# Array halves in turn in the scores and values of two attentions, forget sums added by VectorE, router logits in four column groups, small loads later

## The chip, the cores and the metric

The kernel runs on one core of one Trainium2 chip. Times are device microseconds of one execution, from three runs of the kernel before: the median is 1753.46 us (1751.78 to 1754.30). A profile of one execution gives the rows shown here.

## What is computed

Two transformer blocks on 256 tokens of width 1024, in float32. The first block is a hybrid layer: one projection of the normed input feeds four branches (sliding-window attention "swa" with a relative bias and sinks, a 31-tap convolution, forgetting attention "fox", and block attention "moba" with a relative bias), gated, mixed, and followed by a feed-forward part. The second has a pool branch, a differential attention, a cross attention over 256 memory rows and a mixture of 32 experts of which each token takes four.

```python
# forgetting attention: c is the running sum of log-sigmoid gates
c = jnp.cumsum(log_f, axis=1).transpose(0, 2, 1)
logits = jnp.einsum('bqhd,bshd->bhqs', qi, k) * (HEAD_DIM ** -0.5)
logits = logits + ci[..., None] - c[:, :, None, :]
logits = jnp.where(kpos[None, :] <= qpos[:, None], logits, NEG)
# differential attention: two maps a head, masked by chunks of 64
mask = k_chunk[None, :] <= q_chunk[:, None]
p = jax.nn.softmax(jnp.where(mask, s, -jnp.inf), axis=-1)
a = p[:, :, 0] - lam * p[:, :, 1]
# router
logits = (xt @ w_router + b_router)
top_val, top_idx = lax.top_k(logits, TOP_K)
```

Each of swa, moba and fox has 8 heads of 64 channels, the differential attention 4 heads of two maps with 64 channels each.

## The kernel before

All five engines run programs written out by hand: `tensor_program` (PE), `scalar_program` (ACT), `vector_program` (DVE), `gpsimd_program` (POOL) and `sync_program` (the DMA queue of SP). Each engine works strictly in the order of its program. Between engines there are counting semaphores: `dve["normed", kind, n]` names a step, `q.wait_ge(*...)` waits for it. `Banks` hands out the eight PSUM banks in a fixed turn; `banks.take` waits until the last reader of a bank is through.

Activations lie as channels on partitions, tokens on columns (`h`, `hs`), 8 tiles of 128 x 256. A big weight arrives in "units" of 1 MB (8 x 128 x 256 floats) in four ring slots, issued by SP in the order of the dict `units`, each as soon as PE has finished the unit that held the slot. ACT rounds each unit to a reduced format (`high_r`), DVE computes the rest (`slot_ring_r`, function `rest`), and PE multiplies three times (`thrice`: hi x hi, hi x lo, lo x hi), 48 matmuls of 256 columns a unit. `ahead(name)` on ACT and DVE splits units up to two ahead of the one that PE works on. Scores, values and transposes are plain fp32 matmuls, each of which the trace shows as two records.

The start: ACT issues all 18 loads of small parameter rows (`rows_sb`, L1535), SP loads the identity, x, the first unit, then the constants (L1267, L1268), then further units. POOL issues loads of small inputs. PE transposes x and the rows, norms, and then projects `ub` 0 to 3, `qa` 0 and 1, the forget gate, `ka`/`va`, and q, k, v of moba ("d") and fox ("c").

First attention (`for n in range(8)`): for each head number n PE runs `scores` of swa, moba and fox, a gate unit `gz` 2n, three transposes of each normalised map (`turn_probs`), the unit `gz` 2n+1, and `values` of the three. DVE adds bias or mask (`maxima`, L1896), takes maxima, normalises (`normalise`); ACT takes exponents (`exponents`). Between them DVE does the 31 taps of the convolution and its norm (`conv_step`). A head of 64 channels lies on partitions 0 to 63 or 64 to 127; all three kinds use the same half for the same n. Fox adds its gate sums by a second matmul on two rows (`fox_l` with the sums c, `fox_rt` with -c, rows filled by 16 small DMAs of POOL). POOL also loads a bias matrix `toep` for each swa and moba head from `diag_dram`.

Second block: DVE and ACT norm (`sqrt_table` loads ACT's square-root table), PE projects, rotates, and computes `dscores`: for each head and map m two score matmuls, and after each one a matmul of the identity with the mask `chunk1` that adds it. DVE applies `final_g`, the first block's last norm, to x just ahead of the maxima of the differential attention, and handles the maps one after the other. Then follow `uv`, transposes, pooling, `out2` with its residual (`add_residual`), cross attention, and the router (`wrt`, 8 matmuls into 32 partitions). The experts' weights (12 MB each) come through up to 15 slots; `gate_up` and `down` use 64 columns of the array at a time, in alternating halves, and `scatter` 64 rows at a time.

## Time and profile before

| | us |
|---|---|
| median of three runs | 1753.46 |
| profiled execution | 1753.44 |
| its span, first to last instruction | 1751.6 |
| PE busy in the span | 1607.4 |
| DVE busy | 751.4 |
| ACT busy | 483.4 |
| POOL busy | 166.6 |

The page gives busy time by engine, forty slices of the span with the granted clock of PE and the use of DMA, and the chain of work that ended last. The windows view gives the same for chosen stretches, the timeline single instructions with the idle time before them in square brackets and what ended it. PE is a matmul, PEld a weight load, SPq, ACTq and POOLq the issuing of DMAs. A matmul row shows the array's used rows and columns (64*128: 64 rows, 128 columns), and the size of the moving operand.

### The profile page before, as it was taken

Reading aid. Unit: us, or ns where it says so; the run is one execution under the profiler, and the core shown is the slowest. Engines: PE = TensorE matmul, PEld = TensorE weight load, DVE = VectorE, ACT = ScalarE, POOL = GpSimd, SP = SyncE. Lnnn points to the kernel's source line nnn. Section 1 sums busy time; section 2 is a strip of 40 time slices with the busy share of each in tenths; the row PEclk is TensorE's granted clock in tenths of the full one; section 3 lists DMA queues with packets and bytes.
Section 4 is the critical chain, followed back from the end, with each engine's and each line's share of the span. In section 5 each row is a group of like instructions: output and inputs, shape, how many; then the busy total and the mean of one; then the engine's idle time right before and its main releaser. Section 6 shows DMA issues by size and latency. Waiting matters only on the chain.

```text
span 1751.6 us, 22754 instructions
## 1 busy us (share of the span) xinstructions
PE 1607.4 (92%) x9732; PEld 1015.8 (58%) x9732; DVE 751.4 (43%) x1330; ACT 483.4 (28%) x822; POOL 166.6 (10%) x199
## 2 busy tenths in 40 slices
PE   6999999999999999989999898988888888888885
PEld 6899889989999989984333232323232322323221
DVE  6798765788894678643122121212121212111112
ACT  4445655446554536532011010101010101010001
POOL 1200001503540040110000000000000000000000
PEclk9999999999999999998999999999999999999998
DMA  8754334546655534656999999999999999999994
GB/s 200 204 178 156 117 112 146 167 145 184 183 188 189 179 121 152 221 219 262 405 426 426 426 427 426 425 426 425 426 427 426 426 427 426 426 426 427 427 426 196
DMA packets 194553, 526.44 MB, mean 301 GB/s; under 512 B 18745, under 2 KB 136542, under 8 KB 145294
## 3 DMA queue, kind: packets, MB, share of 16 engines
q1 hardware_dynamic: 190720, 519.34, 76.3%
q0 software_dynamic: 3184, 5.37, 1.6%
q8 instruction: 78, 1.28, 0.3%
q10 hardware_dynamic: 542, 0.21, 0.0%
q14 instruction: 29, 0.24, 0.0%
HBM read 523.24 MB, written 1.61 MB: 300 GB/s over the span
## 4 chain that ended last, share of the span: by engine, by line
PE 43%; DMA 42%; DVE 9%; ACT 3%; issue 1%; SPq 1%; ACTq 1%; DVEq 0%
PE bank L600 42%; DMA slot_ring<-in_w_down 16%; DMA slot_memx<-in_w_down 10%; DMA slot_late<-in_w_down 8%; DMA slot_high<-in_w_down 8%; DVE slot_ring_r L1896 2%; ACT high_r L1479 1%; DVE conv L1904 1%; SPq L1262 1%; ACTq L1535 1%; ACT dscore L1479 0%; DVE rstd L1938 0%; DVE rot_tmp L2330 0%; DMA slot_ring<-in_w_in 0%; DVE x_sb L1904 0%
## 5 line engine op out<-in xcount | busy, mean ns | idle before, releaser
L1896 DVE TENSOR_TENSOR slot_ring_r<-slot_ring,high_r 128x1024 fp32r<-128x1024 f32 x198 | 247.1, 1290 | 96.7 <-ACT high_r L1479 94.2
L600 PE MATMUL bank<-h_hi_r,high_r 128*128 128x256 f32 x1000 | 286.4, 286 | 1.5 <-DVE slot_ring_r L1896 1.3
L600 PE MATMUL bank<-h_lo_r,high_r 128*128 128x256 f32 x1000 | 283.5, 284 | 0.0
L1900 DVE TENSOR_SCALAR ga<-bank 128x512 f32<-128x512 f32 x32 | 22.1, 692 | 579.6 <-PE bank L600 579.6
L600 PE MATMUL bank<-h_hi_r,slot_ring_r 128*128 128x256 f32 x952 | 269.9, 283 | 0.0
L1479 ACT ACTIVATE high_r<-slot_ring 128x1024 fp32r<-128x1024 f32 x198 | 198.0, 1052 | 61.6 <-PE bank L600 42.0
L600 PEld LDWEIGHTS bank<-h_hi_r,high_r 128*128 128x128 f32 x1000 | 191.5, 192 | 4.3 <-DVE slot_ring_r L1896 2.4
L600 PEld LDWEIGHTS bank<-h_lo_r,high_r 128*128 128x128 f32 x1000 | 191.8, 192 | 0.1
L1479 ACT ACTIVATE th_e<-ga 128x512 f32<-128x512 f32 x32 | 20.2, 630 | 612.4 <-DVE ga L1900 612.4
L600 PEld LDWEIGHTS bank<-h_hi_r,slot_ring_r 128*128 128x128 f32 x952 | 182.5, 192 | 0.0
L600 PE MATMUL bank<-slot_ring,xg 128*64 128x512 f32 x528 | 124.6, 604 | 11.7 <-DMA slot_ring<-in_w_gu 11.7
L600 PE MATMUL bank<-slot_high,xg 128*64 128x512 f32 x400 | 94.1, 600 | 7.8 <-DMA slot_high<-in_w_gu 7.8
L1468 POOL CAST bias_of_r<-owners_r 128x128 fp32r<-128x128 f32 x32 | 9.3, 293 | 835.1 <-PE bank L600 835.0
L600 PE MATMUL bank<-slot_ring,hbT 128*64 128x512 f32 x304 | 73.3, 602 | 15.1 <-DMA slot_ring<-in_w_down 15.1
L600 PEld LDWEIGHTS bank<-slot_ring,xg 128*64 128x64 f32 x528 | 34.4, 137 | 88.6 <-issue 51.3
L1900 DVE TENSOR_SCALAR seT_r<-bank,const_sb 128x256 fp32r<-128x256 f32 x32 | 15.5, 484 | 155.1 <-PE bank L600 155.1
L600 PE MATMUL bank<-slot_last,xg 128*64 128x512 f32 x304 | 70.6, 599 | 5.5 <-DMA slot_last<-in_w_gu 5.5
L1479 ACT ACTIVATE hbT<-bank 128x512 f32<-128x512 f32 x32 | 19.1, 597 | 176.0 <-PE bank L1123 176.0
L600 PE MATMUL bank<-slot_late,xg 128*64 128x512 f32 x256 | 61.4, 601 | 5.7 <-DMA slot_late<-in_w_gu 5.7
L600 PEld LDWEIGHTS bank<-slot_high,xg 128*64 128x64 f32 x400 | 25.9, 136 | 66.7 <-issue 38.3
L600 PEld LDWEIGHTS bank<-slot_ring,hbT 128*64 128x64 f32 x304 | 19.9, 136 | 67.5 <-issue 38.4
L600 PE MATMUL bank<-slot_high,hbT 128*64 128x512 f32 x200 | 48.2, 602 | 9.7 <-DMA slot_high<-in_w_down 9.7
(433 smaller groups left out, 2912.1 us busy)
## 6 DMA issues: line engine op xcount, KB each, us to landing
slot_ring<-in_w_gu SPq DMA_DIRECT2D x66, 1024.0 KB, 26.3
slot_high<-in_w_gu SPq DMA_DIRECT2D x50, 1024.0 KB, 26.7
slot_ring<-in_w_down SPq DMA_DIRECT2D x49, 1024.0 KB, 26.5
slot_last<-in_w_gu SPq DMA_DIRECT2D x38, 1024.0 KB, 26.7
slot_ring<-in_w_in SPq DMA_DIRECT2D x36, 1024.0 KB, 5.0
slot_late<-in_w_gu SPq DMA_DIRECT2D x32, 1024.0 KB, 26.4
slot_high<-in_w_down SPq DMA_DIRECT2D x25, 1024.0 KB, 26.9
slot_ring<-in_w_up SPq DMA_DIRECT2D x44, 512.0 KB, 4.5
```

Source lines behind the costliest of these rows:

```text
L600: return e.matmul(o, lhs, rhs, start=start, stop=stop, skip_group_check=True)
L1262: e.dma_start(view(slot_f[slot]), src).then_inc(*slot_in[slot].step("unit", name))
L1468: e.tensor_copy(bias_of[n % 2].rearrange("p (c s) -> p c s", c=2), owners[:, :, n:n + 1].broadcast_to([P, 2, CAP])).then_inc(*pool.step("b ...
L1479: return e.activation(o, i, f, **k)
L1535: e.dma_start(rows_sb[r:r + n, t * P:(t + 1) * P], flat.rearrange("(r p) -> r p", p=P)).then_inc(*rows_ins[t].step("rows"))
L1896: return e.tensor_tensor(o, i, j, op)
L1900: return e.tensor_scalar(o, i, s1, None, op1)
L1904: return e.scalar_tensor_tensor(out=o, in0=i, scalar=s, in1=j, op0=op1, op1=op2)
```

## The change

- **Scores and values, first attention.** One function handles the three kinds of head n. moba uses head n^1, so its half of the partitions is the other one than swa's and fox's. The six score matmuls go in the order swa, moba, fox (256 wide), moba, swa, fox (128 wide), the six value matmuls likewise. The two-row matmuls of fox are gone.
- **Forget sums.** PE transposes the sums to columns (`forget_cols`). POOL stores the negated rows to DRAM (`fox_dram`), loads them for each head broadcast over 128 partitions into one of two buffers `fox_row`, waits for the landing, and adds the causal mask. DVE adds the column and the row in one `scalar_tensor_tensor` in place of the mask's `tensor_tensor`.
- **Differential attention.** Both maps' 256 wide score matmuls, then both 128 wide. The mask matmuls and `chunk1` are gone; DVE writes -1e30 into the unseen quarter of each part in PSUM with one memset a map. The maxima of head n+1 stand ahead of the difference of head n. `final_g` is applied in the `out2` residuals, two of eight tiles ahead of each.
- **Router.** The 8 matmuls go to four groups of 32 partitions, two in each; a matmul with the constant `stack` turns and adds the four.
- **Small loads and steps later.** SP loads the constants ahead of `qa` 0 instead of `ub` 1; the diagonal matmuls come after `qa` 1, their two copies on DVE after the second tap step; POOL's loads of lambda, router and position inputs come after the diagonal stores; ACT spreads the row loads; the rows' second transposes stand between the halves of `ub` 0; ACT's root of `gain_sq` and the square-root table come ahead of the meeting at "block2" instead of behind it.

```diff
@@ scores and values @@
+            def scores(n):
+                for kind in KINDS:
+                    banks.take(q, ("scores", kind, n))
...
+                for kind, i in ((SWA, 0), (MOBA, 0), (FOX, 0), (MOBA, 1), (SWA, 1), (FOX, 1)):
+                    pair, r = n // 2, half_of(kind, n)
...
+                    m = matmul(b[:, c], qt[:, qs], kt[:, ks], True, True)
+                    if i:
+                        m.then_inc(*pe.step("scores", kind, n))
-                for c, qs, ks in ((PARTS[0], slice(128, 256), slice(0, 256)), (PARTS[1], slice(0, 128), slice(0, 128))):
-                    m = matmul(b[:, c], qt[:, qs], kt[:, ks], True, kind != "fox")
-                    if kind == "fox":
-                        m = matmul(b[:, c], fox_pair(fox_l, n)[:, qs], fox_pair(fox_rt, n)[:, ks], False, True)
...
+                for kind, kb in ((SWA, 0), (MOBA, 0), (FOX, 0), (MOBA, 1), (SWA, 1), (FOX, 1)):
+                    r = half_of(kind, n)
+                    o = bank(("heads", kind, pair))[r, 0:S]
...
+                    q.wait_ge(*act["probs", kind, n])
@@ tensor_program, ahead of the q, k, v units @@
+            banks.take(q, "forget columns")
+            q.wait_ge(*dve["forget rows"])
+            for t in range(TT):
+                m = e.transpose(bank("forget columns")[:, t * FOX_H:(t + 1) * FOX_H], zz[:, t * P:(t + 1) * P], ident[0:FOX_H, 0:FOX_H])
@@ differential attention, tensor_program @@
             for head in range(DIFF_H):
+                for c, qs, ks in ((PARTS[0], slice(128, 256), slice(0, 256)), (PARTS[1], slice(0, 128), slice(0, 128))):
+                    for m in range(2):
+                        name, r = ("dscores", head, m), slice(m * HD, (m + 1) * HD)
+                        last = matmul(bank(name)[:, c], uq[r, head, qs], uk[r, head, ks], True, True)
-                        matmul(bank(name)[:, c], uq[r, head, qs], uk[r, head, ks], True, False)
-                        last = matmul(bank(name)[:, c], ident, C("chunk1")[:, cs], False, True)
@@ router @@
-                m = matmul(b[0:NE, 0:S], wrt[:, k, :], h[:, k, :], k == 0, k == KT - 1)
+                m = matmul(b[k % 4 * NE:(k % 4 + 1) * NE, 0:S], wrt[:, k, :], h[:, k, :], k < 4, k >= 4)
-                            m = e.transpose(b[:, S + s * NE:S + (s + 1) * NE], mean_sb[0:NE, s * P:(s + 1) * P], ident[0:NE, 0:NE])
+                            m = matmul(b[:, S + s * NE:S + (s + 1) * NE], mean_sb[:, s * P:(s + 1) * P], C("stack"), True, True)
@@ sync_program @@
-                if name == ("ub", 1):
+                if name == ("qa", 0):
                     e.dma_start(diag_const, a["consts"][:, n_const:]).then_inc(*rest_in.step("rest"))
                     e.dma_start(const_sb[:, 2 * P:], a["consts"][:, 2 * P:n_const]).then_inc(*rest_in.step("rest"))
@@ gpsimd_program @@
+            def fox_rows(n):
+                row = fox_row[n % 2]
+                if n >= 2:
+                    q.wait_ge(*dve["biased", FOX, n - 2])
+                q.wait_ge(*fox_out["fox"])
+                for c, w in ((0, S), (S, P)):
+                    e.dma_start(row[:, c:c + w], fox_dram[n:n + 1, 0:w].broadcast_to([P, w])).then_inc(*fox_ins[n % 2].step("fox", n))
+                q.wait_ge(*fox_ins[n % 2]["fox", n])
...
+                e.tensor_tensor(masked, masked, C("causal")[:, P:2 * P].rearrange("p (c k) -> p c k", c=1).broadcast_to([P, 2, P]),
+                                ALU.add).then_inc(*pool.step("fox", n))
...
                 e.dma_start(toep[n % 8], src).then_inc(*toep_in[n % 8].step("toep", n))
+                if n == 7:
+                    fox_rows(0)
+                    fox_rows(1)
+                elif n >= 9 and n % 2:
+                    fox_rows(n // 2 - 2)
@@ scalar_program @@
+            load_rows(0)
             q.wait_ge(*first_in["first"])
             sqrt_table()
+            load_rows(3)
+            load_rows(2)
...
             for i in (1, 3):
                 evac(("x", i), x[:, 2 * i:2 * i + 2, :], two_of(("x", i)), ("x", i))
+            load_rows(1)
             round_h("ln1_g", range(0, KT // 2))
...
+            sqrt_table()
+            q.wait_ge(*dve["gain squares"])
+            af(gain_sq, gain_sq, ACT.Sqrt).then_inc(*act.step("gain root"))
+            q.wait_ge(*act["gain root"])
             act.mark("block2")
             after_all(q, "block2")
-            sqrt_table()
@@ vector_program @@
-            e.memset(fox_l, 1.0).then_inc(*dve.step())
-            e.memset(fox_rt, 1.0).then_inc(*dve.step())
...
+                    if kind == "fox":
+                        stt(sc[:, c], b[:, c], forget_cols[:, t * FOX_H + n:t * FOX_H + n + 1], fox_row[n % 2][:, c], ALU.add,
+                            ALU.add).then_inc(*dve.step("biased", kind, n))
...
                     ahead((w, i))
+                    if norm == "xattn_g":
+                        q.wait_ge(*act["square", "final_g", 3])
+                        apply("final_g", x, x, steps=(2 * i, 2 * i + 1))
+                        own()
                     q.wait_ge(*pe[w, i])
...
-            q.wait_ge(*act["square", "final_g", 3])
-            apply("final_g", x, x)
...
+            def dmaxima(head):
+                for m in range(2):
+                    b, st = bank(("dscores", head, m)), stats[2 * head + m]
+                    q.wait_ge(*pe["dscores", head, m])
+                    unseen = b[0:CHUNK, P:3 * P].rearrange("p (c k) -> p c k", c=2)[:, :, CHUNK:P]
+                    e.memset(unseen, NEG).then_inc(*dve.step())
+                    own()
...
+            dmaxima(0)
+            for head in range(DIFF_H):
+                if head + 1 < DIFF_H:
+                    dmaxima(head + 1)
+                difference(head)
```

## Rows read from the trace of the kernel before

**Rows 1.** The page: the span.

```profile
span 1751.6 us, 22754 instructions
```

**Rows 2.** Windows: PE, PEld, DVE, ACT, POOL busy (count), granted clock, DMA share, GB/s.

```profile
800.00:805.00 5.00, 4.41 (x28) 2.94 (x30) 3.35 (x14) 1.39 (x3) 0.00 (x0) 1.00 0.01 3
...
837.00:1700.00 863.00, 772.91 (x3544) 263.65 (x3542) 146.12 (x252) 73.58 (x117) 8.71 (x29) 1.00 1.01 426
```

**Rows 3.** The chain that ended last, the start: at us, us long, what.

```profile
8.68 2.32 ACTq L1535
...
20.32 15.26 PE bank L600 x100
...
47.41 6.65 DMA slot_ring<-in_w_in
...
84.14 66.68 PE bank L600 x544
```

**Rows 4.** Timeline of PE, heads 3, 6, 7: start, length, engine, line, out<-in, shapes.

```profile
209.68 0.27 PE L774 MATMUL bank<-const_sb,score_swa 128*128 128x128 f32 x1
...
253.96 0.86 PE L600 MATMUL bank<-prob_swa,va 128*64 128x256 f32 x4
...
256.05 0.70 PE L600 MATMUL bank<-ka,qa 64*128 64x256 f32 x2
...
259.66 0.28 PE L600 MATMUL bank<-h_lo_r,high_r 128*128 128x256 f32 x1
...
284.65 0.27 PE L774 MATMUL bank<-const_sb,score_swa 128*128 128x128 f32 x1
```

**Rows 5.** Timeline of PE in the expert stage: scatter, then gate and up.

```profile
881.88 0.73 PE L600 MATMUL bank<-y_hi_r,seT_r 64*128 64x512 f32 x4
...
882.91 0.39 PE L600 MATMUL bank<-rows_e_r,owners_r 64*128 64x512 f32 x1
...
883.91 1.94 PE L600 MATMUL bank<-slot_memx,xg 128*64 128x512 f32 x8
```

**Rows 6.** Timeline of DVE: last step of heads 0 to 3, first and last of head 4.

```profile
148.71 0.55 DVE L1900 TENSOR_SCALAR score_fox<-score_fox,stat 128x256 f32<-128x256 f32 x2
...
168.08 0.55 DVE L1900 TENSOR_SCALAR score_fox<-score_fox,stat 128x256 f32<-128x256 f32 x2
...
189.12 0.55 DVE L1900 TENSOR_SCALAR score_fox<-score_fox,stat 128x256 f32<-128x256 f32 x2
...
208.05 0.55 DVE L1900 TENSOR_SCALAR score_fox<-score_fox,stat 128x256 f32<-128x256 f32 x2
...
219.51 0.62 DVE L1896 TENSOR_TENSOR score_swa<-bank,toep 128x256 f32<-128x256 f32 x2 [0.49 <-PE bank L600]
...
225.66 0.55 DVE L1900 TENSOR_SCALAR score_fox<-score_fox,stat 128x256 f32<-128x256 f32 x2
```

**Rows 7.** A window in the first attention, columns as in Rows 2.

```profile
240.00:245.00 5.00, 5.00 (x30) 5.00 (x31) 4.16 (x17) 3.79 (x13) 0.00 (x0) 0.66 0.00 0
```

**Rows 8.** DMA issues: out<-in, queue, count, KB each, median us to landing.

```profile
toep<-diag_dram POOLq DMA_DIRECT2D x16, 128.0 KB, 3.1
```

**Rows 9.** Timeline of the differential attention and the out2 stage, PE and DVE.

```profile
637.36 0.70 PE L600 MATMUL bank<-uk,uq 64*128 64x256 f32 x2
...
638.21 3.26 DVE L1904 SCALAR_TENSOR_TENSOR x_sb<-x_sb,cols_sb,rstd 128x256 f32<-128x256 f32 x8
...
653.90 0.37 PE L600 MATMUL bank<-high_r,h_hi_r 128*128 128x256 f32 x1
...
664.23 0.35 DVE L1904 SCALAR_TENSOR_TENSOR dscore<-dscore,stat,dscore 128x128 f32<-128x128 f32 x1
...
697.01 1.52 DVE L1896 TENSOR_TENSOR slot_ring_r<-slot_ring,high_r 128x1024 fp32r<-128x1024 f32 x1 [1.65 <-ACT high_r L1479]
```

**Rows 10.** Timeline of ACT where the second block starts.

```profile
579.32 1.28 ACT L1479 ACT_TABLE_LOAD   x1 [5.65 <-DVE x_sb L1904]
```

**Rows 11.** Timeline of PE, the router.

```profile
787.10 6.52 PE L600 MATMUL bank<-h_sb,wrt 128*32 128x256 f32 x16 [3.14 <-DVE h_sb L1904]
```

## What I predicted, before the change had run

> **What bounds the kernel now.** I read the page first, then the windows, the waits of PE, the chain, and last the timelines of the stages that the change touches. The page gives a span of 1751.6 us [rows 1]; the profiled execution took 1753.44, so 1.84 us lie around the span, and the median of the three runs, 1753.46, is the same number. From 837 us on DMA is busy throughout and moves 426 GB/s while experts are computed [rows 2]: there the end is set by the stream of expert weights, and nothing that PE does in that stretch matters. But the stream can only run ahead as far as there are free slots. At 800 to 805 us DMA stands at 0.01: all slots are full and wait for the router and the first expert [rows 2]. So whatever brings the start of the expert stage forward brings the saturated stream forward by the same, and the end with it. Up to there PE sets the pace: the chain has one piece of PE from 84.14 for 66.68 us and goes on so through the first block [rows 3], and no wait of PE is listed between 140 and 322 us. Before 84 us it is weight loads and VectorE, between 636 and 705 us PE and the softmax chain together. Each part of the change is costed against that.
>
> **Start (moved loads).** ScalarE issues eighteen small DMAs before its first work; the one at 8.68 alone holds its queue for 2.32 us, and PE's first projection starts at 20.32 [rows 3]. After the change eight issues stand ahead, the other ten are spread; six of them (about 0.4 to 0.8 us each in that view) still stand ahead of the rounding of h. SP issues the two constant loads after four weight units instead of after one, and the router's, rotary and lambda loads wait on the POOL queue behind the two diagonal stores. PE's start comes 1 to 3 us earlier. But what comes next in the chain is the DMA of the third unit behind, 6.65 us from 47.41 [rows 3], fed by the 256-byte pieces of the two qa units; the constants now share DMA with these. I take 2.5 us, bounds 0 and 5. The diagonal matmul (1.4 us of PE) and its two copies (1.0 us of DVE) move to the stretch where DVE is late; the two memsets that go (0.96 us) pay for the copies. PE's new wait for "forget rows" before two transposes falls into a gap of 2.6 us that PE has at 82 us anyway; if that cover is gone it costs up to 1.5 us, which is in the bounds. ScalarE's gain root leaves this stage at no cost.
>
> **First attention.** For one head of each kind, values take PE from 253.96 to 256.05, 2.1 us, and scores from 256.05 to 259.5, 3.4 us [rows 4]. By their columns (0.65 us for a 256 and a 128 wide fp32 pair) the scores would be 1.3 us for swa and moba and 1.3 for fox with its two-row matmuls; the 0.8 us more is the switching of fox between 64 rows and 2 rows. The fox matmuls on two rows go altogether, and the six that remain alternate between halves of the array. That halves overlap, rows show: eight 512-column records of y on 64 rows start within 1.03 us, where 0.213 each would be 1.7, and eight records of fp32 on 64 columns take 1.94, where 3.4 would be in sequence [rows 5]. With pairs A, B, A, B, A, A both groups come to 1.28 us; I take 1.45 each for the ends. So PE's own work falls by 2.6 us a head, 21 us in all.
>
> PE will not get all of it. DVE and ScalarE carry a chain from scores to the last normalised fox map of 6.7 us (219.51 to 226.2) [rows 6], and swa's map is now complete 1.07 us after the first score matmul instead of 0.64. In heads 0 to 3 the DVE also does the conv taps and norm: from normalised fox to the next it takes 19.4, 21.0 and 18.9 us (148.71, 168.08, 189.12, 208.05) [rows 6], with hardly a wait for PE, and PE's transposes of head 3 come at 209.68 [rows 4], 1.1 us after the map is ready. So through head 3 only some 1.2 us are gained. From head 4 on the period is 0.4 (rest of the transposes) + 5.7 (48 matmuls) + 1.45 (values) + 1.25 (swa's scores) + 6.7 + 0.1 = 15.6 us; before it was (284.65 - 209.68) / 4 = 18.7 [rows 4], among them three stretches like 240 to 245, where the granted clock is 0.66, partly at 1.2 GHz, right behind half-array matmuls [rows 7]. Four periods give 12.5 us. The last values give 0.7. Against it stand POOL's masks of the fox rows, which share time with DVE: 0.2 us a head, 1.6 us. Together 13 us, bounds 7 and 19. The stt of DVE that adds the column and the row replaces a tensor_tensor of the same shape at the same cost. Behind POOL's new waits for landed rows stand the toep loads of later heads; a toep load lands in 3.1 us [rows 8], POOL adds below 1 us, and each row has over a period of lead, so I cost them at nothing.
>
> On what a switch costs, the dscores show it best: one map there takes 2.07 us on average ((653.90 - 637.36) / 8) [rows 9] for 1.28 us of columns, because each 64-row matmul is followed by one on 128 rows. The Trainium skill, "TensorEngine Tiling (Array Packing)", Key Properties, says that changing the tiling mode drains the array while different tiles of one mode run independently; by it the alternation costs nothing, and its rule agrees with the scatter rows. But the Trainium skill, "TensorE: Matmul & The Clock Gate", Part 3, also says that weight loads overlap running matmuls only where the row group differs; by that the values, which differ in columns alone, would gain nothing, 5 us less. The expert matmuls on 64 columns [rows 5] speak against it.
>
> **Block 2 starts.** At 579.32 ScalarE loads the square-root table for 1.28 us and runs a dummy of 0.1, in the chain, after all engines have met [rows 10]. The change does it before the meeting, where ScalarE has been idle for 5.65 us. Gain 1.4 us.
>
> **Diff attention.** Four things at once. The mask matmuls go: PE needs 0.85 us a head instead of 4.1, 3.4 instead of 16.5 us [rows 9]. DVE no longer applies final_g here (1.75 + 3.26 us at 638.21) [rows 9]. The maxima of the next head run ahead of the difference, so ScalarE's exponents are covered. And two memsets and their waits a head are new on DVE, unseen in this trace: between 0.1 (memset of a small tile) and 0.4 us (a pass over 256 columns), I take 0.2. DVE starts at 638.4, needs 1.8 us for maxima and 2.2 for a difference per head, and ends at 654.4; before it ended at 664.6 [rows 9]. PE gets to uv at 641 and to the transposes at 652.5 instead of 665.5, and waits there for DVE. POOL's pooling starts 3.3 us earlier too and ends at 655.6, just in time. Gain 10.2 us. What is late next is DVE in the out2 stage, where it now has final_g: 1.75 + 8 x 0.42 + three waits, 5.4 us. DVE has idle pieces there such as 1.65 us at 697 [rows 9]; counted unit by unit some 2.6 us are absorbed, and the last residual, on which PE and the next norm wait, comes 2.8 us later. Net 7.4 us, bounds 3 and 11.
>
> **Router.** Eight logical matmuls of 32 columns take 6.52 us [rows 11] at the low clock, while h arrives every 0.41 us. In four column groups the last may start 2.9 us after the first and ends 0.85 later: 2.8 us less, of which I leave 0.5 for a clock that is still low at the transposes behind. Gain 2.3, bounds 0.5 and 3.
>
> **Sum.** 2.5 + 13 + 1.4 + 7.4 + 2.3 = 26.6 us. Span 1725.0, time 1727 us.
>
> **Rivals.** (a) The halves do not overlap for fp32 on 64 rows: every switch of halves costs 0.2 us as in dscores. Scores then take 3.1 us, swa's map is ready 1.5 us later, four periods are 17.1: 6 us less, and 3.5 us less in diff attention: 1736. For it: no fp32 row pair stands in this trace. Against: the scatter. Chance 0.10. (b) The DVE and ScalarE chain gives less than counted, because POOL's masks and the row loads slow DVE, or final_g falls wholly on the out2 stage: 7 us in attention or 5 us in out2: 1734. Chance 0.17. (c) The clock stays at 2.4 GHz in stretches where it fell, and the start gains its 5 us: 1719. Chance 0.12. (d) The kernel gets slower: POOL holds a row pair from "biased" of head n-2 over two loads and an add to head n. Two buffers are in flight, so the period of a head is at least half that path. To lose the 13.6 us of the other parts, eight periods would have to be 1.7 us above today's 18.7, 20.4 us, a path of 41 us. It decides from 31 us on (a period of 15.6). Loads that land in 3.1 us speak against it. At 45 us of path: 1758. Chance 0.02. (e) The stream hides what PE gains, because something ahead of 837 us is bound by DMA after all: within 0.2% of now. Against it: DMA idle at 800. Chance 0.02. The forecast has the remaining 0.57.
>
> **Range and chances.** The unknown costs reach from about 1714 to 1741 if most fall to one side; (a) to (c) lie within that, (d) and (e) outside. A difference of 0.2% is about what a measurement of this kernel can tell. Faster 0.96, same 0.02, slower 0.02.
>
> **What the profile after would show.** Six score matmuls in some 1.4 us; the transposes of head 7 about 16 us before 284.65 with short waits of PE for DVE in front of most fox transposes; no low clock in attention; dscores in under 4 us; the last difference some 10 us nearer to the last upool matmul; DVE without idle time between the out2 residuals; router matmuls in under 4.5 us; the DMA gap at the same depth but earlier. I am wrong if scores still take over 2.5 us, if PE's waits in attention exceed 1 us a head after head 3, if DVE waits for POOL at the fox scores, or if the expert stage starts earlier and the end doesn't follow.

## The result, and the profile of the changed kernel

The changed kernel takes 1744.1 us (median of 7 runs, 1738.2 to 1748.6), the kernel before 1753.9 beside it (7 runs, 1750.8 to 1757.8). The ratio is 0.9946, 95% interval 0.9935 to 0.9958. So it is faster, by 9.7 us or 0.5%, where 26.6 us were forecast, and its time lies outside the range of 1714 to 1741.

The page of the changed kernel, beginning with the span; the last two lines are the DMA engines' busy share and what they moved, in 40 slices of 43.6 us:

```profile
span 1742.7 us, 22667 instructions
...
PEclk9999999999999998999999999999999999999998
DMA  8865455456655544757999999999999999999995
GB/s 221 186 206 146 124 149 169 146 168 183 184 193 179 191 143 136 265 197 291 422 421 421 421 421 421 421 421 421 421 421 422 421 421 423 420 421 422 421 421 216
```

The span is 8.9 us shorter than in [rows 1]. The last line holds the surprise. While the experts are computed the stream moves 420 to 423 GB/s in every full slice, where [rows 2] had 426. The window that answers to the second line of [rows 2] says the same (PE, PEld, DVE, ACT, POOL busy, granted clock, DMA share, GB/s):

```profile
837.00:1700.00 863.00, 761.57 (x3484) 259.02 (x3482) 142.81 (x247) 71.65 (x114) 8.71 (x29) 1.00 1.01 421
```

The DMA share is 1.01 in both: the DMA engines are as busy as before, and each byte takes longer.

The chain that ended last, second block, router and first experts (at us, us long, what):

```profile
591.32 33.09 PE bank L604 x264
...
686.99 31.86 PE bank L604 x244
...
745.66 19.55 PE bank L604 x162
...
770.90 3.61 PE bank L604 x16
...
781.80 18.41 PE bank L604 x82
...
817.22 23.86 PE bank L604 x115
```

The same piece of the first expert (23.86 us, 115 records) began at 834.89 in the kernel before. So the expert stage starts 17.7 us earlier, and the end comes 8.9 us earlier. From that piece to the end of the span it was 1751.6 - 834.9 = 916.7 us; now it is 925.5. Two things have to be explained: 17.7 where 26.6 were forecast, and 8.8 us lost behind that point.

PE in the first attention, head 1: the transposes of its three maps, and the values behind them (start, length, engine, line, operands; in brackets the wait and who ended it):

```profile
163.44 0.30 PE L779 MATMUL bank<-const_sb,score_swa 128*128 128x128 f32 x1 [0.27 <-DVE score_swa L1930]
...
165.31 0.33 PE L779 MATMUL bank<-const_sb,score_moba 128*128 128x128 f32 x1 [1.34 <-DVE score_moba L1930]
...
166.46 0.33 PE L779 MATMUL bank<-const_sb,score_fox 128*128 128x128 f32 x1 [0.60 <-DVE score_fox L1930]
...
168.28 0.58 PE L604 MATMUL bank<-h_hi_r,high_r 128*128 128x256 f32 x1 [1.09 <-ACT gate L1503]
...
176.36 1.89 PE L604 MATMUL bank<-glu,const_sb 128*128 128x256 f32 x8
178.18 0.43 PE L604 MATMUL bank<-prob_swa,va 128*64 128x256 f32 x1
178.19 0.43 PE L604 MATMUL bank<-prob_moba,vd 128*64 128x256 f32 x1
```

Two value matmuls in different halves of the array start 0.01 us apart and run side by side, which is what the change is about. But the transposes wait for VectorE, and from the first fox transpose to the values it takes 11.7 us, where head 2 takes 6.1 (three transposes and 48 matmuls at the full clock). Three things lie in it: a wait of 1.09 us for ScalarE, eight more matmuls, which sum the squares of the convolution for its norm and stand here in head 1 (1.8 us, `glu`), and the clock. Windows of the 5 us before the clock fell and of the 6.8 us in which it was low, of the 5 us steps around them, of one in head 2, and of the end of the out2 stage:

```profile
161.70:166.70 5.00, 2.78 (x15) 1.82 (x14) 4.16 (x17) 3.67 (x14) 1.73 (x3) 1.00 0.92 271
166.70:173.50 6.80, 5.71 (x27) 5.32 (x26) 3.81 (x4) 5.93 (x10) 1.70 (x1) 0.50 0.25 25
...
165.00:170.00 5.00, 3.01 (x14) 2.37 (x15) 4.34 (x9) 4.71 (x10) 0.92 (x2) 0.67 0.68 133
170.00:175.00 5.00, 5.00 (x31) 5.00 (x31) 1.79 (x3) 4.40 (x7) 1.15 (x1) 0.65 0.02 3
190.00:195.00 5.00, 5.00 (x44) 4.96 (x43) 3.84 (x6) 2.53 (x8) 0.53 (x1) 1.00 0.69 226
...
680.00:685.00 5.00, 1.18 (x3) 1.03 (x4) 4.96 (x5) 0.00 (x0) 3.50 (x4) 0.71 0.66 215
685.00:690.00 5.00, 3.88 (x13) 2.80 (x12) 1.63 (x4) 1.19 (x3) 2.68 (x6) 0.50 0.34 101
690.00:695.00 5.00, 5.00 (x35) 5.00 (x35) 4.96 (x11) 2.15 (x6) 0.00 (x0) 0.77 0.00 0
```

Read the PE busy time and the granted clock together. In the 5 us in front of 166.7 PE was busy for 2.78 us, in pieces with waits of up to 1.34 us between them; then the granted clock is 0.50, the lower of its two levels (1.2 of 2.4 GHz), for 6.8 us, into a stretch in which PE has work all the time (170 to 175). The same happens at 680 to 695, with VectorE busy for 4.96 us of the first five. Idle time is not the only thing that a fall follows: in the kernel before the clock falls at 240.0 [rows 7] behind 5 us in which PE was busy throughout:

```profile
235.00:240.00 5.00, 5.00 (x28) 3.50 (x26) 2.33 (x9) 1.26 (x6) 0.00 (x0) 1.00 0.67 210
```

What VectorE of the changed kernel does around 680 us (timeline, as above):

```profile
676.51 2.66 DVE L1926 TENSOR_TENSOR slot_ring_r<-slot_ring,high_r 128x1024 fp32r<-128x1024 f32 x2 [1.64 <-ACT high_r L1503]
...
681.34 3.41 DVE L1926 TENSOR_TENSOR slot_late_r<-slot_late,high_r 128x1024 fp32r<-128x1024 f32 x2
684.68 0.87 DVE L1934 SCALAR_TENSOR_TENSOR x_sb<-x_sb,cols_sb,rstd 128x256 f32<-128x256 f32 x2
685.58 0.69 DVE L1926 TENSOR_TENSOR x_sb<-bank,x_sb 128x512 f32<-128x512 f32 x1
```

The last residual of out2 (685.58) stands behind 3.4 us of splits for a later unit and a pair of final_g steps. It begins 29.6 us behind out2's first matmul (656.01). In the kernel before it was 24.2 us (680.10 to this row):

```profile
704.29 0.68 DVE L1896 TENSOR_TENSOR x_sb<-bank,x_sb 128x512 f32<-128x512 f32 x1
```

PE waits with the sums of the next norm, first for POOL's squares of the residual before it, then for ScalarE's squares of the last:

```profile
683.82 2.05 PE L604 MATMUL bank<-h_sb,const_sb 128*128 128x256 f32 x4 [4.18 <-POOL h_sb L1389]
686.99 2.07 PE L604 MATMUL bank<-h_sb,const_sb 128*128 128x256 f32 x4 [1.12 <-ACT h_sb L1503]
```

### The profile page after: what moved, and what is told of

It is laid out like the page before. It is cut to its first block, busy times and chain, and to the rows that moved or that the text cites. A ratio compares the mean times of both kernels' runs of the same rounds, so it can differ in the third digit from the quotient of the medians.

```text
span 1742.7 us, 22667 instructions
## 1 busy us (share of the span) xinstructions
PE 1574.0 (90%) x9672; PEld 996.7 (57%) x9672; DVE 754.6 (43%) x1337; ACT 482.8 (28%) x822; POOL 179.0 (10%) x208
## 4 chain that ended last, share of the span: by engine, by line
DMA 44%; PE 28%; DVE 6%; ACT 2%; issue 1%; ACTq 0%; DVEq 0%
PE bank L604 27%; DMA slot_ring<-in_w_down 18%; DMA slot_memx<-in_w_down 10%; DMA slot_late<-in_w_down 8%; DMA slot_high<-in_w_down 8%; DVE slot_ring_r L1926 1%; ACT high_r L1503 0%; DVE slot_late_r L1926 0%; DVE rot_tmp L2384 0%; DVE x_sb L1934 0%; DVE mix_lo_r L1926 0%; DVE h_sb L1934 0%; DVE rstd L1968 0%; DVE stat L2341 0%; DVE dscore L1934 0%
## 5 line engine op out<-in xcount | busy, mean ns | idle before, releaser
L604 PE MATMUL bank<-slot_high,hbT 128*64 128x512 f32 x200 | 48.2, 602 | 11.5 <-DMA slot_high<-in_w_down 11.5
```

What stands on the lines that cost most here:

```text
L604: return e.matmul(o, lhs, rhs, start=start, stop=stop, skip_group_check=True)
```

## The experiments

**Is the rate of the stream a matter of the program, and of which part?** Four kernels: both again, and the changed kernel with one placement undone at a time. The change had narrowed the constants, and so moved all SBUF tiles behind them down by 640 bytes, and made the constants' tensor in DRAM 224 columns narrower.

> The kernel before, unchanged, with a second profile. In the first profile the stream of expert weights moved 426 GB/s in every slice from 837 us on; the changed kernel moved 421. Theory P (the rate belongs to the program, by where its tensors lie): again 425 to 427 GB/s and 1753 us. Theory V (the rate differs from one execution to the next, whatever the program): another rate in this profile, between 418 and 430, with a time that goes with it, about 2.1 us for each GB/s (900 us of stream / 426).

Measured: 426 GB/s, 1749.9 us (ratio 0.9993, 0.9982 to 1.0003).

> The changed kernel, unchanged, with a second profile. Theory P: again 420 to 422 GB/s, 1744 us, and the expert stage starts again at 817 us. Theory V: another rate in this profile; at 426 GB/s the same program would take about 1734 us, since 381 MB of stream take 10.6 us less.

Measured: 421 GB/s, 1743.6 us (0.9951, 0.9934 to 0.9967); the piece of the first expert at 816.51.

```diff
-        CONST, COLS = 0, -(-n_const // 8) * 8 + 64
+        CONST, COLS = 0, -(-n_const // 8) * 8 + 224
```

> The changed kernel with every SBUF tile behind the constants moved up by 640 bytes, so that the weight slots lie at the addresses that they have in the kernel before (the narrower constants had moved them down by 640 bytes); nothing else differs. If the placement of the slots in SBUF sets the rate: 426 GB/s and about 1734 us. If it doesn't: 421 GB/s and 1744 us, as the changed kernel beside it.

Measured: 426 GB/s and 1734.3 us (1733.0 to 1735.3; ratio 0.9899, 0.9882 to 0.9915). The window from 1000 to 1600 us, first of the changed kernel:

```profile
1000.00:1600.00 600.00, 521.68 (x2376) 175.81 (x2372) 97.67 (x168) 50.24 (x80) 6.36 (x21) 1.00 1.01 421
```

and of the shifted one:

```profile
1000.00:1600.00 600.00, 528.16 (x2407) 178.09 (x2406) 98.70 (x171) 50.82 (x81) 6.36 (x21) 1.00 1.01 426
```

```diff
+    parts["pad"] = np.zeros((P, 224))
...
-                    e.dma_start(diag_const, a["consts"][:, n_const:]).then_inc(*rest_in.step("rest"))
+                    e.dma_start(diag_const, a["consts"][:, n_const:n_const + 2 * TOEP]).then_inc(*rest_in.step("rest"))
```

> The changed kernel with the constants in DRAM padded by 224 unused columns to the width they have in the kernel before, 2051 columns (the change had narrowed them by 112 KB in all); nothing else differs. If the place of the weights in DRAM, moved by the narrower constants, sets the rate: 426 GB/s and about 1734 us. If it doesn't: 421 GB/s and 1744 us.

Measured: 421 GB/s, 1743.7 us. So the rate belongs to the program, not to the execution, and it hangs on the place in SBUF, not in DRAM. That alone is 9 to 10 us.

**Which alignment?** The first tile stands at byte 16512 of each partition, and the ring slots 10432 columns of 4 bytes behind it in the changed kernel, 10592 in the kernel before: byte 58240 (384 above a multiple of 512) and byte 58880 (on a multiple). The high slots follow them and start alike. Seven more slots are anchored at the end of SBUF and start 384 bytes above a multiple of 512 in both.

> The changed kernel with all tiles behind the constants moved up by 128 bytes instead of 640. The four ring slots and the three high slots then start at a multiple of 512 bytes (they start 384 bytes above one in the changed kernel, and on one in the kernel before). Theory A (a slot's start against a multiple of 512 bytes sets the rate of its loads): 426 GB/s in the expert stage, as in the kernel before, and about 1734 us. Theory B (the absolute place in SBUF, or what lies beside what): not 426 again, some other value at or near 421, 1744 us.

Measured (`+ 96` for `+ 64`): 426 GB/s, 1734.0 us in a single run. This and the other placements that give one time and no interval were run once; the rate is what they are read by, and it was 421 in every profile of the changed kernel.

> The changed kernel with all tiles behind the constants moved up by 384 bytes: ring and high slots then start 256 bytes above a multiple of 512. Theory A with 512 bytes: 421 GB/s, 1744 us. Theory A with 256 bytes or less: 426 GB/s, 1734 us. Theory B: a third value.

Measured (`+ 160`): 426 GB/s, 1733.5 us. For ring and high slots a start 256 bytes above a multiple of 512 is as good as one on it; what is bad is 128 bytes above a multiple of 256.

```diff
-        CONST, COLS = 0, -(-n_const // 8) * 8 + 64
+        CONST, COLS = 0, -(-n_const // 8) * 8 + 184
...
-        RING0 = POSI + S + 32
+        RING0 = POSI + S + 72
...
-        AREAS = 53184 - AR
+        AREAS = 53088 - AR
```

> The changed kernel with all fifteen slots at multiples of 512 bytes: ring and high slots as after the shift by 640 bytes, the seven slots at the end of SBUF moved down by 384 bytes (they start 384 bytes above a multiple of 512 in both kernels of the case), and the slot in the normalised activations moved as well. In the window from 1000 to 1600 us ring and high slots took 113 of some 240 loads of 1 MB; their alignment was worth 5 GB/s. Theory A: the other slots give as much for their share, 5 x 127 / 113 = 5.6 GB/s more, 432 GB/s; 381 MB of stream then take 882 us instead of 905, and the kernel some 1721 to 1723 us. Rival (426 GB/s is the ceiling of the transfers, or only the slots that VectorE and ScalarE split matter): 426 GB/s and 1734 us.

Measured: 427 GB/s and 1734.5 us (1733.1 to 1734.6; ratio 0.9884, 0.9856 to 0.9911). My sum of 432 GB/s falls: the second half of the slots gives almost nothing. The rival's numbers are met; which of its two readings holds, the run on the slots at the end shows below.

**Which tiles?** Three gaps. In front of the ring slots (`RING0 = POSI + S + 64`):

> The changed kernel with 128 bytes of gap in front of the ring slots alone: constants, x, h, the normalised activations and the small tiles stay where they are, the ring and high slots and the area behind them move up by 128 bytes. If the start of ring and high slots, or of the area behind them, sets the rate: 426 GB/s, 1734 us. If it is the place of the tiles in front (x and h, which hold the gathered rows of the experts, and one slot in the normalised activations): 421 GB/s, 1744 us.

Measured: 426 GB/s, 1731.8 us. The tiles in front moved, the slots not:

> The reverse: the tiles in front of the ring slots move down by 128 bytes, and the gap of 128 bytes behind them leaves the ring and high slots and the area behind them where the changed kernel has them. If ring and high slots set the rate: 421 GB/s, 1744 us. If the tiles in front do: 426 GB/s, 1734 us.

Measured: 421 GB/s, 1744.4 us. Only the seven slots at the end on good starts (`AREAS = 53088 - AR`), with ring and high slots left where they are:

> The changed kernel with only the seven slots at the end of SBUF moved down by 384 bytes, to a multiple of 512; ring and high slots stay 384 bytes above one. Theory G (a load into a slot that starts off a multiple of 256 bytes costs the DMA engines more; the memory behind allows 426 GB/s, so half of the loads on good starts is enough): 426 GB/s and 1734 us, as with the ring and high slots alone moved. Theory R (only ring and high slots matter, since they hold the split weights, or since of what lies behind them): 421 GB/s and 1744 us.

Measured: 426 GB/s, 1732.9 us. And a gap behind the high slots:

> The changed kernel with 128 bytes of gap behind the high slots: only the area behind them (token rows, tables, products of the experts, no weight slots) moves. If the slots' own start sets the rate, as the two runs with gaps in front of them leave open: 421 GB/s, 1744 us. If the area behind does: 426 GB/s, 1734 us.

Measured: 421 GB/s; its time was 1738.9 us in the one run, with the first expert's piece already at 812.63 (a fast first half), and from there 924.5 us to the end, as in the changed kernel. So it is the start of the weight slots themselves, and either half of them is enough; that only the slots with split weights matter is refuted. The bytes in the 600 us window rank the four mixes. Changed kernel, no slot on a multiple of 256:

```profile
DMA packets 34749, 252.70 MB, mean 421 GB/s; under 512 B 3859, under 2 KB 3859, under 8 KB 3987
```

ring and high slots on one (gap_before_ring):

```profile
DMA packets 35149, 255.61 MB, mean 426 GB/s; under 512 B 3903, under 2 KB 3903, under 8 KB 4031
```

all fifteen on one (all_slots_512):

```profile
DMA packets 35205, 256.02 MB, mean 427 GB/s; under 512 B 3909, under 2 KB 3909, under 8 KB 4037
```

The end slots alone also moved 255.61 MB. None costs 1.3% against all, half costs 0.2%.

**Does it hold without the change?** The kernel before, moved by 384 bytes:

```diff
-        CONST, COLS = 0, -(-n_const // 8) * 8
+        CONST, COLS = 0, -(-n_const // 8) * 8 + 96
```

> The kernel before with everything behind the constants moved up by 384 bytes, so that its ring and high slots start 384 bytes above a multiple of 512 bytes, as in the changed kernel. If the placement alone took the gain away: 421 GB/s in the expert stage, 369 MB from 837 us on take 10 us more, 1763 to 1764 us. If something else of the change belongs to it: 426 GB/s, 1753 us.

Measured: 1762.9 us (1761.1 to 1763.9; ratio 1.0056, 1.0039 to 1.0073), and

```profile
1000.00:1600.00 600.00, 521.86 (x2380) 176.16 (x2378) 98.39 (x170) 50.26 (x80) 6.37 (x21) 1.00 1.01 421
```

The placement alone slows the kernel before by as much as it took from the changed one.

**Do the halves of the array overlap, and what is it worth?**

```diff
-            return n // 2 + 4 * (n % 2) if kind == SWA else n ^ 1 if kind == MOBA else n
+            return n // 2 + 4 * (n % 2) if kind == SWA else n
...
-            i = (n + (kind == MOBA)) % 2
+            i = n % 2
```

> The changed kernel with moba's heads in the same half of the array as swa's and fox's, so that no two of the six score matmuls and no two of the value matmuls that follow each other lie in different halves; order and number as in the changed kernel. Theory H (the halves overlap, and this gave part of the gain in attention): scores take 2.0 us a head instead of 1.5 and values 2.0 instead of 1.5; heads 4 to 7 are bound by PE and get 1 us longer each, heads 0 to 3 hardly, 4 to 5 us in all: 1748 us, and the expert stage starts at 821 us. Rival (only the fox matmuls on two rows that went were worth anything): scores and values as in the changed kernel within 0.2 us, expert stage at 817, 1744 us.

Measured: 1747.9 us (ratio 0.9972, 0.9956 to 0.9988), the first expert's piece at 820.95 instead of 817.22. Values and scores of head 5, first in the changed kernel (PE):

```profile
247.28 0.43 PE L604 MATMUL bank<-prob_swa,va 128*64 128x256 f32 x1
247.29 0.43 PE L604 MATMUL bank<-prob_moba,vd 128*64 128x256 f32 x1
...
248.73 0.48 PE L604 MATMUL bank<-ka,qa 64*128 64x256 f32 x1
248.73 0.48 PE L604 MATMUL bank<-kd,qd 64*128 64x256 f32 x1
```

and with the same halves:

```profile
248.13 0.65 PE L604 MATMUL bank<-prob_swa,va 128*64 128x256 f32 x2
248.61 0.59 PE L604 MATMUL bank<-prob_moba,vd 128*64 128x256 f32 x2
...
250.23 0.70 PE L604 MATMUL bank<-ka,qa 64*128 64x256 f32 x2
250.76 0.59 PE L604 MATMUL bank<-kd,qd 64*128 64x256 f32 x2
...
252.38 0.39 PE L604 MATMUL bank<-h_hi_r,high_r 128*128 128x256 f32 x1
```

Values take 1.45 us (247.28 to 248.73) against 2.10, scores 1.5 against 2.15. From the first score of head 0 to the values of head 7 it is 138.1 us against 142.9, and 147.0 in the kernel before. Theory H holds, for rows and for columns. The kernel before had 2.1 us for values and 3.4 for scores [rows 4]: what the scores gain beyond the halves comes from the two-row matmuls that went.

**What does PE's idle time in heads 1 and 3 cost?** Fill-in matmuls, whose product nothing reads:

```diff
-            def turn_probs(name, src, ready):
+            def turn_probs(name, src, ready, filler=0):
                 banks.take(q, name)
+                for j in range(filler):
+                    matmul(bank(name)[:, 0:256], hs.hi[:, j % 8, 0:P], hs.hi[:, (j + 1) % 8, :], True, True)
...
+                               filler={"swa": 8, "moba": 13, "fox": 6}[kind] if n in (1, 3) else 0)
```

> The changed kernel with 27 matmuls of 256 columns in heads 1 and 3 of the first attention, placed where PE waits for the three normalised maps (8, 13 and 6; 0.11 us each at 2.4 GHz); they write into the bank that the transposes overwrite. In the changed kernel the 48 matmuls behind the transposes of head 1 take 11.5 us at a granted clock of 0.65 (5.9 us in head 2 at 1.00), those of head 3 7.0 us. Theory C (the clock falls because PE stands still between the transposes, and this costs what the gain in scores and values had brought in heads 0 to 3): the clock stays at 1.00 there, values of head 1 begin 5 us earlier, the expert stage 5 to 6.5 us earlier, at 811, and the kernel takes 1738 us. Rival (PE is held up by its operands there, whatever the clock): values of head 1 begin at 178 as before, 1744 us or somewhat more.

Measured: 1740.3 us (1738.0 to 1741.0; ratio 0.9916, 0.9887 to 0.9945), and

```profile
165.00:170.00 5.00, 4.04 (x35) 3.80 (x34) 3.68 (x4) 4.13 (x7) 1.73 (x1) 1.00 0.33 25
170.00:175.00 5.00, 5.00 (x37) 4.22 (x37) 2.36 (x2) 4.96 (x8) 0.00 (x0) 1.00 0.31 85
205.00:210.00 5.00, 5.00 (x45) 5.00 (x44) 3.15 (x6) 3.91 (x9) 0.84 (x1) 1.00 0.31 55
```

The clock stays at 1.00 through the whole first attention, as theory C says. But from the fox transposes to the values of head 1 it is still 9.0 us (11.7 without the fill-in), of head 3 6.1 (7.5). So the clock cost 2.7 + 1.4 us and not 6; the first score to the last values shrink by 3.2 us (138.1 to 134.9), and the time by 3.3 (against 1743.6). The first expert's piece begins at 814.5, not at the 811 of theory C. I had read all of head 1's 11.7 us as 48 matmuls and their clock. What is left above 6.1 us is a wait of 0.96 us for ScalarE's `gate` which the kernel before doesn't have, and the eight matmuls of the convolution's norm, 1.8 us, which it has (7.9 us in the same place).

**What does final_g cost in the out2 stage?** Put back ahead of the diff attention:

> The changed kernel with final_g applied ahead of the diff attention again, as in the kernel before, and not between the residuals of out2. In the changed kernel the time from the start of out2's matmuls to the first product of the next norm's projection is 40.1 us (32.3 in the kernel before). Theory F (final_g in front of the residuals costs these 7.8 us, through VectorE and through the low clock of the wait): the diff attention starts 5 us later, the stretch behind it is 7 to 8 us shorter, the expert stage starts 2 to 3 us earlier, 1741 us. Rival (PE only catches up with VectorE's splits there, and final_g costs the 2.8 us that were forecast or less): the stretch shrinks by under 3 us and the expert stage starts 2 us later or more, 1746 us.

Measured: the stretch from out2's first matmul to that of `co` (the output projection of the cross attention) is 81.6 us (659.44 to 741.01), 8.1 shorter; the diff attention in front is 6.2 us longer (the first out2 matmul 292.8 instead of 286.6 us behind the start of the feed-forward piece). The stretch shrinks as theory F says, and by these marks 1.9 us are gained in all. The median, 1743.6 us (1739.7 to 1744.7), lies between theory and rival and doesn't show it, so the sign of the whole stays open. Applied in one go behind the diff attention instead:

```diff
                 after_all(q, NORM_START[norm])
+                if norm == "xattn_g":
+                    q.wait_ge(*act["square", "final_g", 3])
+                    apply("final_g", x, x)
+                    own()
                 for i in range(4):
                     xs = x[:, 2 * i:2 * i + 2, :]
                     ahead((w, i))
-                    if norm == "xattn_g":
-                        q.wait_ge(*act["square", "final_g", 3])
-                        apply("final_g", x, x, steps=(2 * i, 2 * i + 1))
-                        own()
```

> The changed kernel with final_g applied to all eight blocks in one go behind the diff attention, before the first split of the out2 stage, where VectorE waits 2.7 us for ScalarE, instead of in pairs between the residuals. With final_g ahead of the diff attention the stretch from out2's first matmul to co's took 81.6 us, with the pairs 89.7. Theory F (what costs is that each pair stands behind the splits of a unit, in front of a residual): the stretch falls by 4 us or more, to under 86 us, and the diff attention stays as early as in the changed kernel; expert stage 4 us earlier, 1740 us. Rival (VectorE is full there whatever the order): the stretch stays at 88 to 90 us, 1744 us.

Measured: the stretch is 87.2 us (653.90 to 741.09), the time 1740.6 us (1737.3 to 1743.4). Neither of the two bounds is met. The last residual says what the order does: it begins 28.0 us behind out2's first matmul, where the pairs had 29.6 and the kernel before 24.2. So the order gives 1.5 us, and VectorE being full keeps the rest. The other 0.9 us of the stretch go with the clock, which was low there for 3.4 us in this profile and for 10.2 in the first of the changed kernel; the next kernel has the same order, the same 28.0 us, 6.8 us of low clock, and a stretch of 89.0.

**All together, and one move more.**

> All that was found, in one kernel: the changed kernel with all slots at multiples of 512 bytes (1734.45 us alone), the fill-in matmuls in heads 1 and 3 (3.3 us less alone) and final_g applied in one go behind the diff attention (3.0 us less alone). Theory: the three act at different places and add up: 1744.0 - 9.6 - 3.3 - 3.0 = 1728 us, with 427 GB/s and the expert stage from 810 us on. Rival (starting the expert stage earlier is worth nothing once the stream is bound by DMA from there): 1734 us.

Measured: 1731.0 us (1730.7 to 1735.6; ratio 0.9873, 0.9857 to 0.9890), 427 GB/s. It is 3 us more than the sum and 3 less than the rival, and the profile misses the forecast in one more point: the first expert's piece begins at 816.9, not from 810 on. The fill-in matmuls gave their 3 us in heads 0 to 3 (74.6 us for 77.4); the out2 stretch stayed at 89.0; and the feed-forward piece of PE takes 206.2 us with all slots aligned, 203.4 in the changed kernel (and 202.6 with the gap in front of the ring alone); why wasn't tested. That the three add up is not shown.

```diff
-                    ahead((w, i))
+                    if i < 3 or norm != "xattn_g":
+                        ahead((w, i))
...
+                    if i == 3 and norm == "xattn_g":
+                        ahead((w, i))
```

> The same with one more move: in the out2 stage VectorE adds the last residual before it splits the unit ahead of it, not behind. In the changed kernel the last residual stands at 685.6 us behind 3.4 us of splits, while PE waits for the norm. Theory: PE's wait shrinks by up to 3 us and the low clock behind it comes earlier or not at all: 1725 to 1726 us. Rival (the splits that now come later are what the projection behind the norm waits for): 1728 us, as the other one.

Measured: 1727.6 us (1727.2 to 1729.6; ratio 0.9858, 0.9841 to 0.9876), faster than both kernels of the case. The absolute number is nearer to the rival's, but the move is worth 3.4 us against the kernel without it, as the theory has it. The last residual begins 25.7 us behind out2's first matmul instead of 28.0, the stretch from out2 to co is 83.8 us instead of 89.0, and the low clock behind the wait is gone:

```profile
680.00:685.00 5.00, 4.37 (x32) 3.95 (x30) 4.06 (x6) 1.31 (x3) 3.15 (x5) 1.00 0.43 129
685.00:690.00 5.00, 5.00 (x44) 4.97 (x43) 4.82 (x9) 2.07 (x5) 2.13 (x5) 1.00 0.83 274
```

## Why the prediction was wrong

From marks in the two first profiles, in us (gain positive):

| step | forecast | measured |
|---|---|---|
| start: first score of head 0 at 141.53, then 138.13 | 2.5 | 3.4 |
| heads 0 to 3: first score to the values of head 3, 74.9, then 77.4 | 1.2 | -2.5 |
| heads 4 to 7: on to the values of head 7, 72.2, then 60.7 | 12.5 | 11.5 |
| last values, masks, on to the start of the feed-forward piece (382.56, then 369.41) | -0.7 | 0.8 |
| from there to the first dscores: second block starts | 1.4 | 0.8 |
| diff attention: first dscores to out2, 42.7, then 32.6 | 10.2 | 10.2 |
| out2 to co, 81.8, then 89.7 | -2.8 | -7.8 |
| router to the first expert's piece, 47.8, then 46.3 | 2.3 | 1.5 |
| **expert stage starts** | **26.6** | **17.7** |
| expert stage itself, 916.7, then 925.5 | 0 | -8.8 |
| **end of the span** | **26.6** | **8.9** |

The table has one profile of each kernel, and the clock falls at other places in every profile. In the second profiles the expert stage starts at 833.0 and 816.5, 16.5 us earlier, and takes 914.5 and 925.2 us. So in the second pair the rate costs 10.7 us. The first pair has 8.8; there the kernel before had the clock low for 6.9 us near its end, which the second profile doesn't have:

```profile
1724.80:1731.70 6.90, 6.21 (x16) 1.75 (x17) 0.00 (x0) 0.60 (x1) 0.00 (x0) 0.51 0.23 97
```

**The step that failed most** is the sentence that whatever brings the expert stage forward brings the saturated stream and the end forward by the same. Its mechanism stands: with the slots on good starts (gap_before_ring) the stage takes 1730.0 - 815.2 = 914.8 us, as in the kernel before (914.5 from 833.0 on). What I took for granted is that the rate of [rows 2] stays. The change narrows the constants and pads them by 64 columns, and I read these lines of the diff as mere room; the weight slots moved with them. No rival had this. Rival (e) expected the stream to hide PE's gain by being the bound ahead of 837 us; that is not what happened. With the rate restored and nothing else, the changed kernel takes 1734 us, inside the range, though 7 us above the forecast, for which the next two steps stand.

**Attention.** The overlap of the halves was right to the tenth: 1.45 us for scores and values forecast, 1.5 and 1.45 measured, and a period of 15.9 us in heads 4 to 7 for 15.6. Rival (a) is refuted by same_halves. What failed is heads 0 to 3. I had them bound by VectorE and ScalarE, which they are, and concluded that PE's gain there is worth nothing. It is worth less than nothing: the time that PE saves becomes idle time between transposes, the clock falls behind it, and the matmuls behind pay for it. With PE kept busy by the fill-in the four heads take 74.2 us instead of 77.4, which gives back 3.2 of the 3.7 us by which the term was off. The kernel before had low stretches in these heads too, 3.4 us in its first profile and 6.8 in its second, against 10.2 in both of the changed kernel; so the loss is 2.5 us in the first pair of profiles and 1.3 in the second (76.4, then 77.7). My own sign, no low clock in attention, was wrong in heads 1 and 3 and right from head 4 on.

**Diff attention and final_g.** The memset on PSUM takes 0.17 us (0.2 assumed), and the gain of 10.2 us is met. What failed is "counted unit by unit some 2.6 us are absorbed". VectorE absorbs nothing: the last residual comes 5.4 us later behind out2's first matmul (29.6 for 24.2), all of the 5.4 that final_g was costed at, where 2.8 were forecast; and 2.4 us more pass from it to co, where the clock is low for 10.2 us behind PE's wait and was not low before. That makes the 7.8. The 1.65 us of idle time in [rows 9] are a wait for ScalarE's half of the split, and the changed kernel still has it, 1.64 us at 676.51. This is rival (b) in its second form, price and all (5 us in out2).

**Start and router.** The start gave more than its term; in the other profiles of the changed kernel the first score stands between 135.5 and 138.9, in those of the kernel before at 141.1 to 141.5. The router's sixteen matmul records fell from 6.52 us [rows 11] to 3.61, as forecast. What that is worth can't be told: from there to the first expert's piece it takes 43 to 48 us in the profiles, and the kernel before has both ends (47.8 and 43.3). The clock was low for 12.7 us of the 47.8 and for 3.4 of the 43.3.

**Two slips in the working.** In rival (d) a path of 45 us gives a period of 22.5, and by the rival's own rule eight periods 3.8 us above 18.7, less 13.6, are 17 us more and a time of 1770, not 1758. The parts of the attention term add up to 12.8, not 13. Together they move the forecast by 0.2 us.

On the overlap of values, which differ in columns alone: the Trainium skill, "TensorE: Matmul & The Clock Gate", Part 3, says that weight loads overlap running matmuls only where the row group differs. The runs disagree for this form: values with alternating column halves take 1.45 us against 2.10, and the trace has weight loads that start and end while a matmul on the same 128 rows runs, as this one during the value matmul that starts at 247.28 and takes 0.43 us:

```profile
247.34 0.14 PEld L604 LDWEIGHTS bank<-prob_swa,va 128*64 128x64 f32 x1
```

## What to carry to other kernels

Before costing a change at a DMA-bound kernel, compute where every DMA destination starts, before and after: a padding constant or a removed table moves all tiles behind it, and 128 bytes decided some 10 us here. And where PE is not the bound, a faster PE is not free: idle time between short matmuls can be followed by a low clock in the dense piece behind it (3.2 us here), so fill the gap or shift VectorE's work out of it. When work moves into a stage because an engine "has gaps" there, check that the gaps are not waits that stay. And read the low-clock stretches of both profiles before putting a difference of 1 or 2 us in a stage down to an edit.

## What was not expected of the hardware

The rate of 1 MB loads into SBUF hangs on the start of the destination in each partition. With no slot on a multiple of 256 bytes (fourteen of the fifteen lie 128 bytes above one, the last 32) 252.7 MB pass in 600 us; with all on a multiple of 512 it is 256.0. With half of them good, starts 256 bytes above a multiple of 512 do as well as starts on one (426 GB/s in both). Other starts weren't tried.

The Trainium skill, "DMA: Bandwidth & Descriptors", "How a descriptor splits into AXI transactions", says that a transaction must start from a 256-byte-aligned address, and that the bytes in front of a run that starts elsewhere are fetched and still cost beats of 32 bytes. The page words this for bytes that are fetched; here it is the destination that starts off the boundary. The trace agrees on the boundary and about on the size: for runs of 8 KB, 128 bytes above it, an estimate from that page is 4 beats more on 256, 1.6%, and the runs show 1.3%. They disagree on the mixture: with half of the slots off, the page's rule would give half of the loss, and the runs show 0.2%. That something else limits the stream near 426 GB/s, and hides the loss until nearly all loads have it, fits the rate in all twenty profiles, but it wasn't tested by itself.
